# Splits of the attention operands made with the projections, stacked score operands, and three smaller changes in a two-layer hybrid transformer kernel

## The reference

```python
dk = rms_norm(dk..., da_k_norm)          # and dq; both rotated for latent tokens
k  = concat([rms_norm(k_nope), rope(rms_norm(kr)) broadcast over heads])
q  = concat([rms_norm(q_nope), rope(rms_norm(q_rope))])
def apply_axial_rope(x, cos, sin):       # pairs 16 rows apart in each 32
    y1 = x1 * c - x2 * s
    y2 = x2 * c + x1 * s
s = einsum(q * DA_DIM ** -0.5, k)        # diff_attention, c = 0, 1 (two halves)
p = softmax(s);  (p[:, 0] - lam * p[:, 1]) @ v
s = einsum(q * 192 ** -0.5, k)           # softmax_attention
softmax(s) @ v
```

## Time and profile before

| | |
|---|---|
| median of three runs | 2865.18 us (2862.68 to 2867.93) |
| the profiled execution, its own time | 2866.67 us |
| its span in the trace | 2864.9 us |
| mean granted TensorE clock | 0.962 of full speed |
| PE busy | 2657.4 us, 93% |
| PE weight loads, beside PE | 2191.3 us, 76% |
| DVE busy | 1327.5 us, 46% |
| ACT busy | 1088.4 us, 38% |
| POOL busy | 894.9 us, 31% |
| moved by DMA | 284.16 MB, mean 99 GB/s |

### The profile page before, as it was taken

The page is one execution under the profiler, slowest core; times in us unless marked ns, Lnnn a source line. Parts: engine busy times, 40 slices in busy tenths (PEclk is TensorE's granted clock), DMA queues, the critical chain, the costliest instruction groups (busy, mean ns, idle before and its releaser), DMA issues.

```text
span 2864.9 us, 41511 instructions
## 1 busy us (share of the span) xinstructions
PE 2657.4 (93%) x15904; PEld 2191.3 (76%) x15904; DVE 1327.5 (46%) x2089; ACT 1088.4 (38%) x1891; POOL 894.9 (31%) x413
## 2 busy tenths in 40 slices
PE   7999999777679799999999999999989998899999
PEld 5888888675665588888888876889766665788887
DVE  4877784565757632344334344221566662311111
ACT  4444422546366432321221234342656665322221
POOL 2222222534436412223222223122311106334443
PEclk9999999888789899999999999999999998999999
DMA  7344454103020131232332322213532201222222
GB/s 275 112 132 132 132 188 168 67 24 122 24 89 1 43 127 53 94 127 98 124 129 95 115 77 85 96 63 104 183 127 68 68 21 59 88 79 98 103 88 88
DMA packets 111712, 284.16 MB, mean 99 GB/s; under 512 B 10320, under 2 KB 37456, under 8 KB 110160
## 3 DMA queue, kind: packets, MB, share of 16 engines
q1 hardware_dynamic: 89536, 235.50, 24.2%
q10 hardware_dynamic: 22032, 46.67, 4.6%
HBM read 238.22 MB, written 43.91 MB: 98 GB/s over the span
## 4 chain that ended last, share of the span: by engine, by line
PE 70%; issue 14%; DVE 8%; ACT 4%; POOL 3%; DMA 1%; ACTq 0%; SPq 0%; POOLq 0%; DVEq 0%
PE ps L546 16%; PE ps L547 16%; PE ps L548 16%; PE ps L1332 3%; PE ps L1287 2%; POOL Wl L525 2%; PE ps L1318 2%; PE ps L1296 2%; PE ps L1240 1%; PE ps L1030 1%; DVE ps L2563 1%; DVE Vall L2567 1%; PE ps L1211 1%; PE ps L1212 1%; PE ps L1213 1%
## 5 line engine op out<-in xcount | busy, mean ns | idle before, releaser
L525 POOL TENSOR_TENSOR Wl<-raws,Wh 128x2048 fp32r<-128x2048 f32 (+3 forms) x138 | 593.7, 4302 | 1429.0 <-ACT Wh L519 1429.0
L546 PE MATMUL ps<-Hh,Wh 128*128 128x512 f32 (+1 forms) x1792 | 623.5, 348 | 20.7 <-POOL Wl L525 15.9
L547 PE MATMUL ps<-Hl,Wh 128*128 128x512 f32 (+1 forms) x1792 | 615.7, 344 | 0.0
L548 PE MATMUL ps<-Hh,Wl 128*128 128x512 f32 (+1 forms) x1792 | 609.9, 340 | 0.0
L546 PEld LDWEIGHTS ps<-Hh,Wh 128*128 128x128 f32 x1792 | 340.6, 190 | 71.4 <-issue 24.0
L547 PEld LDWEIGHTS ps<-Hl,Wh 128*128 128x128 f32 x1792 | 340.5, 190 | 40.8 <-issue 2.9
L548 PEld LDWEIGHTS ps<-Hh,Wl 128*128 128x128 f32 x1792 | 339.0, 189 | 42.4
L519 ACT ACTIVATE Wh<-raws 128x2048 fp32r<-128x2048 f32 (+3 forms) x140 | 247.5, 1768 | 238.8 <-PE ps L548 197.1
L2493 DVE SCALAR_TENSOR_TENSOR ybuf<-ubuf,vec,ybuf 128x770 f32<-128x770 f32 x144 | 204.2, 1418 | 57.2 <-ACT ybuf L1550 41.9
L2878 DVE TENSOR_TENSOR hdb<-sgb,ps 128x768 f32<-128x768 f32 (+1 forms) x44 | 36.1, 821 | 365.5 <-PE ps L548 365.5
L2801 DVE SCALAR_TENSOR_TENSOR xT<-ps,mod,xT 128x512 f32 (+1 forms) x82 | 52.2, 663 | 311.3 <-PE ps L548 310.9
(11 more groups left out here) (399 smaller groups left out, 5150.3 us busy)
## 6 DMA issues: line engine op xcount, KB each, us to landing
raws<-in_slabs SPq DMA_DIRECT2D x234, 512.0 KB, 4.1
adl<-in_ada ACTq DMA_DIRECT2D x48, 512.0 KB, 3.8
ada<-in_ada SPq DMA_DIRECT2D x32, 512.0 KB, 4.4
chunks<-obuf ACTq DMA_DIRECT2D x52, 256.0 KB, 3.3
ada<-in_ada SPq DMA_DIRECT2D x8, 1024.0 KB, 4.8
chunks<-obuf ACTq DMA_DIRECT2D x52, 128.0 KB, 3.2
chunks<-ebuf SPq DMA_DIRECT2D x17, 384.0 KB, 2.6
raws<-in_slabs SPq DMA_DIRECT2D x16, 384.0 KB, 3.7
```

What stands on the lines that cost most here:

```text
L525: nc.gpsimd.tensor_tensor(Wl[n % 2][:, 0:w], raw[n % 2][:, 0:w], Wh[n % 2][:, 0:w].bitcast(f32), ALU.subtract).then_inc(sig("slab_lo"), 1)
L546: nc.tensor.matmul(o, lhs(c)[0], rhs(c, t0, t1)[0], start=(s == 0), stop=False)
L547: nc.tensor.matmul(o, lhs(c)[0], rhs(c, t0, t1)[1], start=False, stop=False)
L548: last = nc.tensor.matmul(o, lhs(c)[1], rhs(c, t0, t1)[0], start=False, stop=(s == k - 1))
```

## The change

Five parts:

1. Each of the 37 units is split where it is made: two loops later ACT copies its high part (`unit_high`, to `uh`) and DVE subtracts the low part (`unit_low`, to `ul`). SP stores both (`chunks` and `lows`), each after its own semaphore, and the ring's place is free once the subtraction is done. The high copies (ACT) and low subtractions (POOL) of the attention turns are gone.
2. The score operands are stacked over 128 rows. DA: `das` holds a query's high part over its low part (swapped for b=1), `dak` the key's high part twice, so one pass gives high x high and low x high; `dal` holds the key lows, and 64-row passes (`rest`) add high x low. An ML item's plain part is three fp32r passes (`mqh`, `mql`, `mkh`, `mkl`), and its rotated part one stacked pass (`mrs`, `krh`) and one 64-row pass (`krl`). A DA item is 4 full and 4 rest passes, an ML item 16 full and 4 rest passes. SP loads per half of a turn 9 transfers for DA, 6 for ML and 2 for values, 17 for 8 before, 3968 KB for 2304 KB. The first ones are issued in uq1 (10 transfers where 3 were) and in ukv1 (9 where 4 were).
3. Rotation: the permutation matrix and its product are gone; DVE swaps rows 16 apart with `stream_shuffle` into bank 5, the gain comes swapped (`V_SWAP`), the sign stands in the sine table.
4. in0: ACT copies the high half of the next body's first slab ahead of the last two SiLUs of the body before.
5. SSD: direction 1 of slots 11 and 12 reads its state into bank 1 or 2; ACT's squares (slots to 11) and DVE's `finished` (slots to 12) move to the end of their slot.

```diff
-        out[r, C_SIN:C_SIN + LAT] = np.sin(ang)
+        out[r, C_SIN:C_SIN + LAT] = np.sin(ang) if r % 32 >= 16 else -np.sin(ang)
 
...
+        def read_bank(slot, d):
+            return slot - 10 if d and slot >= 11 else 5
...
+        def read_free(slot, d):
+            if (slot, d) == (11, 1):
+                return "sd_gm", past("sd_gm") + 4 * NT
+            if (slot, d) == (12, 1):
+                return "sd_m", past("sd_m") + 4 * NT
+            g, k = SUNITS[slot]
+            n = READS.index((g, k, d)) - (slot == 12)
+            return "ss_acc", past("ss_acc") + n
...
                 pe.wait_ge(sig("ss_s"), past("ss_s") + UPDATES.index((g, k - 1, d)) + 1)
                 if n:
-                    pe.wait_ge(sig("ss_acc"), past("ss_acc") + n)
+                    name, count = read_free(slot, d)
+                    pe.wait_ge(sig(name), count)
                 for j in range(4):
-                    ins = nc.tensor.matmul(ps[:, 5, j * P:(j + 1) * P], hst[g][d][:, j * P:(j + 1) * P], sC[g][:, tc], start=True, stop=True)
+                    ins = nc.tensor.matmul(ps[:, read_bank(slot, d), j * P:(j + 1) * P], hst[g][d][:, j * P:(j + 1) * P], sC[g][:, tc], start=True, stop=True)
                 ins.then_inc(sig("ss_ch"), 1)
...
-            if kind == "unit" and UNITS[m][4] is not None:
-                _, _, _, _, r, rv = UNITS[m]
-                if rv == 0:
-                    pe.wait_ge(sig("un_mat"), 4)
-                pe.wait_ge(sig("un_raw"), m + 1)
-                if rv:
-                    pe.wait_ge(sig("un_sin"), rv)
-                nc.tensor.matmul(ps[:, 5, :], rotg[:, r, :], ebuf[e % 4][:, 0:LAT], start=True, stop=True).then_inc(sig("un_rot"), 1)
...
+                four = ((1, 0, 256, b0 + 1, 256), (0, 0, 512, b0, 0), (0, 512, T, b0 + 1, 0), (1, 256, T, b0 + 2, 0))
+                if kind == "da":
+                    def full(b, tq, t0, t1):
+                        return ((das[hh][:, b, tq], dak[hh][:, b, t0:t1]),)
+                    def rest(b, tq, t0, t1):
+                        rows = slice(64 * b, 64 * b + 64)
+                        return das[hh][rows, b, tq], dal[hh][rows, t0:t1]
                 else:
...
+                    def full(b, tq, t0, t1):
+                        qh, ql, kh, kl = (t[hh] for t in (mqh, mql, mkh, mkl))
+                        return ((qh[:, tq], kh[:, t0:t1]), (qh[:, tq], kl[:, t0:t1]), (ql[:, tq], kh[:, t0:t1]),
+                                (mrs[hh][:, tq], krh[:, t0:t1]))
...
+                    def rest(b, tq, t0, t1):
+                        return mrs[hh][0:64, tq], krl[0:64, t0:t1]
+                def queries(b):
+                    return slice(x * P, (x + 1) * P) if kind == "da" else slice((2 * x + b) * P, (2 * x + b + 1) * P)
+                for b, t0, t1, bank, c in four:
+                    for y, (q, k) in enumerate(full(b, queries(b), t0, t1)):
+                        nc.tensor.matmul(ps[:, bank, c:c + t1 - t0], q, k, start=(y == 0 and (b, t0) != (0, 512)), stop=False,
+                                         skip_group_check=True)
+                for y, (b, t0, t1, bank, c) in enumerate(four):
                     if y == 2:
+                        pe.wait_ge(sig("at_half"), past("at_half") + 12 * i + n + 1)
+                    q, k = rest(b, queries(b), t0, t1)
+                    ins = nc.tensor.matmul(ps[:, bank, c:c + t1 - t0], q, k, start=False, stop=True, skip_group_check=True)
+                    if y == 0:
                         ins.then_inc(sig("at_half"), 1)
...
-                if not gates:
-                    hi_slab(act, n0 + 1, i, before=4 * i + c0)
...
+                hi_slab(act, n0 + 3, i, before=4 * i + c0 + 4)
...
-            loop(act, 4, gate_body)
+            gate_body(0, False, True)
+            loop(act, 4, gate_body, 1)
...
-                for y, x in enumerate(SFIN.get(i, ())):
+                for y, x in enumerate(SFIN.get(i, ()) if i > 11 else ()):
                     squared(x)
...
+                for x in SFIN.get(i, ()) if i <= 11 else ():
+                    squared(x)
             act.wait_ge(sig("ss_t"), past("ss_t") + 20)
...
-                    if n in (2, 4):
...
-                        (high_da if n == 2 else high_ml)(i, 1)
...
+                x = STORED[e - 4]
+                if x[3] == "unit":
+                    eng.wait_ge(sig("un_lo"), past("un_lo") + x[4] + 1)
+                else:
+                    eng.wait_ge(sig(f"ustore{e % 4}"), 16 * rows_stored(e - 4))
...
+            def unit_high(x):
+                if x[3] != "unit":
+                    return
+                m, e, w = x[4], STORED.index(x), chunk_width(x)
+                act.wait_ge(sig("un_done"), m + 1)
+                high_free(act, m)
+                nc.scalar.activation(uh[m % 2][:, 0:w], ebuf[e % 4][:, 0:w], ACT.Copy).then_inc(sig("un_hi"), 1)
...
+                if q > 1:
+                    unit_high(QKV[q - 2])
...
                 dve.wait_ge(sig("ss_ch"), past("ss_ch") + n + 1)
                 dve.wait_ge(sig("ss_ec"), past("ss_ec") + n + 1)
-                nc.vector.tensor_tensor(ps[:, 5, :], ps[:, 5, :], ecs[n % 2][:, :], ALU.mult).then_inc(sig("ss_t"), 1)
+                b = read_bank(slot, d)
+                nc.vector.tensor_tensor(ps[:, b, :], ps[:, b, :], ecs[n % 2][:, :], ALU.mult).then_inc(sig("ss_t"), 1)
                 dve.wait_ge(sig("ss_t"), past("ss_t") + n + 1)
...
                     kept(i + 2)
-                for y, x in enumerate(SFIN.get(i - 2, ())):
+                for y, x in enumerate(SFIN.get(i - 2, ()) if i > 12 else ()):
                     finished(x)
                     for c in LOWS.get((i, y), ()):
...
                 grown(i, 1)
+                for x in SFIN.get(i - 2, ()) if i <= 12 else ():
+                    finished(x)
...
                     q, t0 = usin, LAT
-                    dve.wait_ge(sig("un_rot"), rv + 1)
...
+                    dve.wait_ge(sig("un_raw"), m + 1)
+                    if rv:
+                        dve.wait_ge(sig("un_sin"), rv)
+                    nc.vector.stream_shuffle(ps[:, 5, :], v[:, 0:LAT], [lane ^ 16 for lane in range(32)]).then_inc(sig("un_rot"), 1)
                     if m:
                         dve.wait_ge(sig("un_done"), m)
-                    nc.vector.tensor_tensor(q[:, :], ps[:, 5, :], sin, ALU.mult).then_inc(sig("un_sin"), 1)
+                    dve.wait_ge(sig("un_rot"), rv + 1)
+                    nc.vector.scalar_tensor_tensor(q[:, :], ps[:, 5, :], vec[:, V_SWAP + r:V_SWAP + r + 1], sin, ALU.mult, ALU.mult)\
+                        .then_inc(sig("un_sin"), 1)
                     nc.vector.scalar_tensor_tensor(ucos[:, :], v[:, 0:LAT], vec[:, gain:gain + 1], cos, ALU.mult, ALU.mult)\
...
+                if x[3] != "unit":
+                    return
+                m, e, w = x[4], STORED.index(x), chunk_width(x)
+                dve.wait_ge(sig("un_hi"), past("un_hi") + m + 1)
+                high_free(dve, m)
+                nc.vector.tensor_tensor(ul[m % 2][:, 0:w], ebuf[e % 4][:, 0:w], uh[m % 2][:, 0:w].bitcast(f32), ALU.subtract)\
+                    .then_inc(sig("un_lo"), 1)
...
                     for e in (unit_store(16), unit_store(17), unit_store(25), unit_store(29)):
                         stored(sp, e)
                     for half in range(2):
-                        sp.dma_start(mkrr[64 * half:64 * half + 64, :], scr["chunks"][36, 0:64, :]).then_inc(sig("mkr_in"), 16)
+                        sp.dma_start(krh[64 * half:64 * half + 64, :].bitcast(f32), scr["chunks"][36, 0:64, :]).then_inc(sig("kr_in"), 16)
+                    sp.dma_start(krl[0:64, :].bitcast(f32), scr["lows"][36, 0:64, :]).then_inc(sig("kr_in"), 16)
                     heads_ml(sp, 0, 0)
                 if n == S["ukv1"][0] + 4:
...
+        def head_rows(name, row, n, w):
...
+            for b in range(2):
+                for half in range(2):
+                    rows = slice(64 * half, 64 * half + 64)
+                    sp.dma_start(das[hh][rows, b, :].bitcast(f32), head_rows(("chunks", "lows")[half ^ b], row + 64 * b, 64, LAT)).then_inc(sig(f"da_in{hh}"), 16)
+                    sp.dma_start(dak[hh][rows, b, :].bitcast(f32), head_rows("chunks", row + 8 * P + 64 * b, 64, T)).then_inc(sig(f"da_in{hh}"), 16)
+            sp.dma_start(dal[hh][:, :].bitcast(f32), head_rows("lows", row + 8 * P, P, T)).then_inc(sig(f"da_in{hh}"), 16)
         def heads_ml(sp, i, hh):
...
-                sp.dma_start(mrr[64 * half:64 * half + 64, :], rows64[ds(24 * P + 128 * i + 64 * hh, 64), 0:LAT]).then_inc(sig("at_q1"), 16)
+            row = 2 * P * i + P * hh
+            for half, name in enumerate(("chunks", "lows")):
+                sp.dma_start((mqh, mql)[half][hh][:, :].bitcast(f32), head_rows(name, row + 16 * P, P, LAT)).then_inc(sig(f"ml_in{hh}"), 16)
```

(8 more changed lines are left out.)

176 lines of the change are left out of this document (54 added, 122 removed).

## The result

The changed kernel takes 2839.2 us, the median of four runs (2836.4 to 2842.6), against 2865.0 for the kernel before: 0.991 of its time, 95% interval 0.989 to 0.993, or 26 us less. That is outside the range of 2795 to 2838, and half of the 53 us that were forecast.

| stretch | before, us | after, us | change | forecast |
|---|---|---|---|---|
| start to in0's loop | | | -1.2 | 0 |
| in0, from 107 to 399 us | 291.4 | 284.9 | -6.6 | -14 |
| DeltaNet | | | -2.8 | 0 |
| SSD, to out0's second product | 149.8 | 141.1 | -8.7 | -14 |
| qk1, lat1, dv1 (17 rotated units) | | | -14.5 | -14.6 |

The account below looks back on a forecast made before the run. The prediction took PE as the bound, 70% of the chain of waits. Its terms, -14 -14 -18 +3 +7 -7 -11 +1 = -53, took 2866.7 to 2813.7, less 1.5 for the median's scale 2812 us; range 2795 to 2838.

Parts of the forecast that it names:

- Splits and SP's queue: In uq1 and ukv1, added copies, stores and head-load issues cost +4.5 for ukv1 and +2.5 for uq1: +7, bounds 0 and +20.
- the splits clog uq1 and ukv1: Rival: a unit's copy, subtraction and two stores form a line longer than its period; 15 to 20 us more, chance 0.14.
- Rotation: In rotated units, 21 PE products of 0.86 us go: -18; DVE takes over with a shuffle assumed at 0.6 us.
- DVE's +3: Four rotated ML units in a row: 5.0 us on DVE against 3.62 on PE, ring hiding about half; bounds 0 and +8.
- In0: In in0, moving ACT's high copy into its idle 5.09 us removes PE's waits for POOL: -14, bounds 0 and -16.
- SSD: In SSD, waits at state reads go through new banks and later squares: 8 + 4 + 2, -14, bounds -4 and -22.
- The squares and slot 2: In SSD, 4 us for slot 10's wait behind late squares and 2 for slot 2's half-hidden wait.
- Attention: Stacked score passes save 0.23 us on each of 32 DA items (-7) and 0.68 on 16 ML items (-11); DVE's jitter +1.
- The pairs: In attention scores, 64-row passes on the two halves of the rows run side by side, 0.23 us a pair, 0.46 for two.
- the same 0.3: In a DA item's scores, the unchanged time for filling the array and for `at_half`, within a forecast 1.46 us.
- DVE's margin: In attention, DVE's 3.95 us against PE's 4.01, margin about 0.06; rival that DVE takes over: +9, 2821, chance 0.12.
- the slower rival: Rival: PE thins out in attention and its clock falls to 0.80; +64, 2876 us, chance 0.04.

Follow-up runs that it names:

- heads_spread: The changed kernel with the first attention head loads issued two at a time behind each slab load, not in a row ahead of one; 2827.6 us.
- slabs_later: heads_spread with out1's two slab loads issued after ukv1's loop instead of among its last stores; 2823.1 us.
- heads_narrow: The changed kernel with its 19 early head loads cut to 64 columns, whole loads after ukv1; ACT's slab waits 5.1 and 2.6 us, for 7.7 and 5.6.
- ml_rot_pe: The changed kernel with the four rotated ML query units swapped by a PE product again, all others by the shuffle; 2837.3 us.
- silu_moved: The changed kernel with the last SiLU of an in0 body on ACT moved behind the next body's first eviction; 2825.9 us.
- bank5: The changed kernel with direction 1 of SSD slots 11 and 12 read into bank 5 again; 2841.7 us.
- order_undone: The changed kernel with ACT's squares and DVE's `finished` back at the start of their SSD slots, banks 1 and 2 kept; 2843.5 us.
- rest_order: The changed kernel with the last two of an item's four 64-row passes exchanged, so `at_half` is waited for before the last only; 2834.8 us.
- together_full: together with key lows on both halves of the rows, all attention passes over 128 rows and no `at_half` wait; 2792.2 us.
- together: The changed kernel with the edits of heads_spread, slabs_later, ml_rot_pe and silu_moved in one; 2806.7 us.

## Why the prediction was wrong

- **Splits and SP's queue** is the step that failed: +7 for uq1 and ukv1, with bounds 0 and 20; together with the other terms there +6.6 was forecast and +22.6 measured. It said that "slabs are fetched several ahead, so most is covered". They are fetched one ahead, into two buffers; that is plain in `load_slab` and was not looked up. ACT stood 13.3 us for two slabs. The 0.42 to 0.5 us an issue came from a row of slab loads; behind a transfer to 64 rows an issue takes 0.58 to 0.60. heads_spread gives 11.7 us back and slabs_later 3.6 more, and heads_narrow shows the issues and the bytes as parts. The rival "the splits clog uq1 and ukv1" named the place and a size of 15 to 20 us (16 came), but another mechanism: it had the line of copy, subtraction and stores as too long. That line carries a unit in 3.62 us in heads_spread.
- **Rotation.** -18 for PE's products: 17 of 21 came as worked out, 14.5 us. The shuffle takes 0.69 us, for 0.60 taken, and the seven operations 4.85, for 5.0. But DVE's +3 assumed that the ring hides half; it hides none, since each unit's square stands on DVE behind the chain of the unit before. ml_rot_pe puts it at 3.0 us for leaving the four on PE, so that with the 3.4 us of the products DVE cost 6.4 there.
- **In0.** -14 was forecast, -6.6 came. The wait for POOL went as worked out; what was late next was not asked. The 5.09 us of idle ACT in the earlier trace rows were read as room, and are ACT waiting in order, with PE's banks behind it. silu_moved shows the rest, and more than the 8 us.
- **SSD.** -14 forecast, -8.7 measured. The banks were priced at 8, the longest wait, and gave 4.0 (bank5). The squares and slot 2 were priced at 6 and gave 6.9 to 7.5 (order_undone). That makes the 11.3 gained up to out0's first product, and 2.6 were lost again because the products behind it ran at a clock of 0.53, where it had been 1.00; the prediction had no such term.
- **Attention.** -17 forecast, -17.4 measured, by other terms, so that the agreement is luck. DA: -7 forecast; the item went from 1.70 to 1.74, +1. ML: -11 forecast, -5 (4.37 to 4.06). DVE: +1 forecast, -5: the waits for its probabilities are gone, and they were POOL's doing, of which the prediction said that it does not count. The work between two items' scores became 0.17 to 0.18 us shorter at every place, some 8 us in all, for which there was no term. By single passes, that time went where the scores begin: from the last pass of the values to the first of the scores were 0.205 us ahead of DA and 0.215 ahead of ML, and are 0.03 now. Ahead of DA the change from 128 to 64 rows stood there and lies inside the item now. Ahead of ML both passes have 128 rows before and after; what changed is that the first score product was a plain fp32 one and is an fp32r pass, and no run separates that.
- **The pairs** of 64-row passes did run side by side: the first two of an item start 0.003 us apart and so do the last two (medians of 32 DA items). But the second pair starts 0.44 us behind the first (2169.66 and 2170.10 above), where a pass of 512 columns takes 0.23. So the wait of `at_half` is bare by 0.2 us: from the pass that it waits for to the pass behind the wait are 0.44 us, and only one other pass stands between them. Before, these were 0.46 (2191.58 to 2192.04), and other passes filled them. The prediction had the wait in "the same 0.3". rest_order takes 0.11 of it away. Beside the columns there are further the 0.09 into 64 rows and 0.18 (ML 0.09) out of them, which together_full saves too. The Trainium skill, "TensorEngine Tiling (Array Packing)", in its key properties, also says that changing the tiling mode drains the engine; the prediction cited the page for the parallel tiles alone, which stand there too, and the trace agrees with both.
- **DVE's margin** of 0.06 us was no threshold. The 3.95 us are the chain of the second of two DA items, behind which PE has about 3.9 us of other work ahead of ML's scores; the 2.54 us it was compared with stand behind the first, whose chain is 3.24 (2170.63 to 2173.87 in DVE's timeline of the changed kernel). In together_full the two together, 2.3 and 1.49, are still over 3.24, and PE waits 0.5 us in all.
- The clock kept at 0.98 in attention and fell to 0.93 to 0.95 in uq1 and ukv1, as PE waited there; the slower rival did not come.

What stays open: DeltaNet's -2.8 us was in no forecast. Nothing was changed there, and its offsets vary by 2 us among the runs; none was made for it. uq1 and ukv1 still take 93.0 us in together, where they took 87.5 before, though the four products are back on PE and the head loads no longer stand in a row ahead of the slabs; no run shows what holds these 5.5. Why the clock fell at out0's start was not tested either.

## What to carry to other kernels

Before a row of transfers goes into a queue, look at what stands behind it and how many buffers that has: ten issues of 0.6 us ahead of a load that is fetched one ahead cost more than the bytes. An idle engine is room only if it isn't the one that frees another's banks next; ask what stands behind the wait. Price a removed wait by the next wait on the same way, not by its length. And when work leaves an engine that is not the bottleneck, look in the trace at what ran beside it and took longer than usual.
